# A PEER trunk layer on one core: the residual stage folded into the last expert group, four rows per group re-timed, and the gate-table stores issued by ScalarE

## The chip, the cores and the metric

One Trainium2 chip, one of its cores. The metric is device time in microseconds of one execution of the whole layer. TensorE (PE), VectorE (DVE), ScalarE (ACT), GpSimd (POOL) and SyncE (SP) run their own instruction streams and meet at semaphores; the 16 DMA engines move data between SBUF and DRAM.

## The reference, cut to what matters

The layer has two sub-layers. The first (two token mixers, merge, output projection) gives `x1`. The second is a PEER retrieval layer, and it is the one that the change touches:

```
h2   = rms_norm(x1) * (1 + scale2) + shift2
s    = (h2 @ w_query) . sub_keys           # 8 heads, 2 halves, 128 keys each
16 best of 16 x 16 sums per head -> experts, gate = softmax
act  = gelu(h2 . expert_u[experts])
y    = sum over the 128 chosen experts of gate * act * expert_v[expert]
out  = x1 + gate2 * y
```

There are 1024 tokens, D = 1024, and 16384 experts (128 x 128). `x1`, `out` and both expert tables are float32.

## The kernel before, in words

The 1024 tokens are 8 tiles of 128. Six of them (`DT` = 6, 768 tokens) are computed **densely**: for all 16384 experts, with a gate matrix that is zero where an expert was not chosen. The last two tiles (`FEW` = 2) are computed **sparsely**: each chosen expert's row is fetched by an indirect DMA (a gather of one 1024-wide row per token, 512 KB), in a ring of four buffers (`RING` = 4), 256 gathers of expert_u rows and 256 of expert_v rows.

**rows_phase (U part).** For each of 128 expert rows, PE multiplies the row's 128 experts with the 768 tokens (two halves, L534 to L536), ACT applies Gelu (L1623) into one buffer per half, and SP stores each half into the table `ahead` in DRAM (`Ahead.store`, L1590 to L1594). ACT may write a half's buffer again only when its store has landed (`ge_out`, L1620). Cutting of float32 operands into a high and a low part is done by ACT (`cut_high`, L1613) and DVE (`cut_low`, L1617); the row's expert_u is loaded by POOL (L1588), and POOL also issues the sparse gathers (L1539), whose dot products DVE takes (`dot_row`, L1556). DVE runs its steps in the order in which they are written: the low cut of the next row, then the dot products.

The phase has three stages, each with two rows or so per step: `tiles` (48 rows, routing beside them), `blocks` (24 rows in 12 blocks of 64 tokens) and `rest` (56 rows; the first 23 turns of two rows bring one batch of four gathers per row). In `blocks` the gate matrix is built: per group of four tokens DVE (L1913, L1917) and ACT (`last_row`, L1780, L1782) write one-hot rows, PE multiplies them (L1985), ACT copies the result to `stage` (L1805). After 16 groups the block's 4 MB, 16384 runs of 256 bytes, go to the DRAM table `gates` in one DMA (L1764). SP issues it, after the block's last two stores of `ahead`:

```
for j in range(ROWS_BLOCK):
    A.store(sp, ...)
sp.wait_ge(g_cp.sem, g_cp.done(b * NG + (NG - 1)))
sp.dma_start(gv[...], stage[...]).then_inc(st_out[half].sem, 16)
```

**expert_phase (V part).** 32 groups of four expert rows. Per group PE runs 12 units (6 token tiles x 2 halves of D), 12 matmuls each (L2147 to L2149). The even units add up in six held PSUM banks over all groups; the odd units go through two moving banks that DVE adds to `acc` (L2119). DVE also multiplies the next group's two tables (`gate`, L2097), cuts (`cut_v` L2101, `cut_H` L2105) and adds eight gathered rows per group (`add_row`, L1565) at the units of `ROW_AT`, every unit but 2, 5, 8 and 11. POOL gathers the rows. SP loads `expert_v`, `ahead` and `gates` (L2056, L2058, L2060). After the last group ACT copies the six held banks to `acc` (L2089).

**finish_phase.** A phase of its own: SP loads gate2 (broadcast, 512 KB) and the 8 tiles of x1, DVE multiplies and adds tile by tile (L2184, L2186; `Chain` makes each wait for the one before), SP stores each tile (L2176). Phases are separated by a barrier of all engines and the clearing of semaphores.

## Time and profile before

| what | us |
|---|---|
| median of 3 runs | 3766.74 |
| lowest and highest run | 3756.76, 3779.36 |
| the profiled execution, its own time | 3757.52 |
| its span, first to last instruction | 3755.6 |

Mean granted TensorE clock of the profiled execution: 0.953 of full speed. Busy shares of the span: PE 90%, DVE 69%, ACT 31%, POOL 23%.

How to read it: a row of the timeline is start, duration, engine, line of the kernel, operation, output <- inputs, count and, in brackets, the idle time before it and what ended it. "SPq" and "POOLq" rows are the issuing of DMAs, not the transfer. A table by stage gives, for each stretch, each engine's busy time, the granted clock, the DMA engines' mean share and GB/s.

### The profile page before, as it was taken

The page shows a single profiled execution, that of the slowest core. Times are in us where ns is not written, and L with a number is a line of the kernel's source. Part 1 is how long each engine was busy: PE and PEld are TensorE (multiplying, and loading weights), DVE is VectorE, ACT ScalarE, POOL GpSimd, SP SyncE. Part 2 cuts the span into 40 slices and gives each one's busy share as a digit, 9 for nine tenths or more (in the row PEclk, how much of TensorE's full clock was granted, in tenths as well). Part 3 has the DMA queues.
Part 4 walks back from the last instruction along what each step waited for, and adds up shares of the span by engine and source line. Part 5 has one row for each costly group of instructions (what it writes and reads, how often), then busy time and mean ns, then how long its engine had stood idle before and what let it go on. Part 6 is the DMA issues. An engine that isn't in the chain of part 4 may idle for free. (4 is left out here: it accounts for less than half of the span.)

```text
span 3755.6 us, 58665 instructions
## 1 busy us (share of the span) xinstructions
PE 3374.4 (90%) x18867; PEld 3068.5 (82%) x18867; DVE 2585.7 (69%) x4897; ACT 1174.2 (31%) x1966; POOL 873.0 (23%) x900
## 2 busy tenths in 40 slices
PE   5997999786579699999999899999699999999996
PEld 4997999774468599999899899999588888888885
DVE  6435777444358788888888756663577777777775
ACT  3004555321222223226777522222222222222220
POOL 1001111110000001112222257662233333333331
PEclk8998999897789899999999999999899999999998
DMA  6622222242211134445888999994687778778775
GB/s 248 218 88 93 88 88 73 93 125 88 84 54 44 37 123 142 151 155 160 236 235 238 262 308 342 337 332 175 243 296 288 284 287 295 283 283 294 289 284 196
DMA packets 436327, 745.41 MB, mean 198 GB/s; under 512 B 224304, under 2 KB 275680, under 8 KB 433120
## 3 DMA queue, kind: packets, MB, share of 16 engines
q1 hardware_dynamic: 337312, 375.61, 30.1%
q0 software_dynamic: 98304, 368.10, 28.3%
q8 instruction: 68, 1.11, 0.1%
q14 instruction: 67, 0.55, 0.0%
q10 hardware_dynamic: 576, 0.04, 0.0%
HBM read 610.44 MB, written 133.19 MB: 198 GB/s over the span
## 5 line engine op out<-in xcount | busy, mean ns | idle before, releaser
L534 PE MATMUL apab<-h2hi,auhib 128*128 128x384 f32 x2048 | 707.1, 345 | 65.5 <-DVEq L60 47.1
L536 PE MATMUL apab<-h2hi,aulob 128*128 128x384 f32 x2048 | 687.3, 336 | 0.0
L535 PE MATMUL apab<-h2lo,auhib 128*128 128x384 f32 x2048 | 687.3, 336 | 0.0
L1539 POOL DMA_INDIRECT vrow<-in_expert_v,fw_now x256 | 318.1, 1242 | 723.8 <-DVE acc L1565 710.7
L534 PEld LDWEIGHTS apab<-h2hi,auhib 128*128 128x128 f32 x2048 | 387.3, 189 | 75.4 <-ACT ageb L1623 36.6
L535 PEld LDWEIGHTS apab<-h2lo,auhib 128*128 128x128 f32 x2048 | 387.3, 189 | 0.0
L536 PEld LDWEIGHTS apab<-h2hi,aulob 128*128 128x128 f32 x2048 | 386.2, 189 | 0.0
L1623 ACT ACTIVATE ageb<-apab 128x384 f32<-128x384 f32 x256 | 125.7, 491 | 686.9 <-PE apab L536 663.5
L2147 PE MATMUL eheld<-vhi,Hhi 128*128 128x512 f32 x768 | 303.0, 395 | 32.4 <-DVE Hlo L2105 32.4
L1565 DVE SCALAR_TENSOR_TENSOR acc<-vrow,fw_share,acc 128x1024 f32<-128x1024 f32 x256 | 327.2, 1279 | 0.0
L1588 POOL DMA_DIRECT2D aurb<-in_expert_u x128 | 71.6, 560 | 1033.6 <-DVEq L60 709.6
L2119 DVE TENSOR_TENSOR acc<-acc,evo 128x512 f32<-128x512 f32 x192 | 132.1, 688 | 255.8 <-PE evo L2149 255.8
L2148 PE MATMUL eheld<-vlo,Hhi 128*128 128x512 f32 x768 | 300.1, 391 | 0.0
L2149 PE MATMUL eheld<-vhi,Hlo 128*128 128x512 f32 x768 | 299.4, 390 | 0.0
L2147 PE MATMUL evo<-vhi,Hhi 128*128 128x512 f32 x768 | 298.8, 389 | 0.0
L2148 PE MATMUL evo<-vlo,Hhi 128*128 128x512 f32 x768 | 298.8, 389 | 0.0
L2149 PE MATMUL evo<-vhi,Hlo 128*128 128x512 f32 x768 | 298.7, 389 | 0.0
L2081 ACT ACTIVATE Hhi<-gr 128x768 fp32r<-128x768 f32 x128 | 108.5, 848 | 604.6 <-DVE gr L2097 604.6
L1985 PE MATMUL gp<-grow,gcol 128*128 128x128 f32 x1536 | 208.6, 279 | 31.5 <-ACT grow L1782 16.4
L1985 PEld LDWEIGHTS gp<-grow,gcol 128*128 128x128 f32 x1536 | 198.3, 193 | 42.9 <-issue 28.8
L1617 DVE TENSOR_TENSOR aulob<-aurb,auhib 128x1024 fp32r<-128x1024 f32 x128 | 156.5, 1223 | 110.5 <-ACT auhib L1613 107.1
L1556 DVE SCALAR_TENSOR_TENSOR urow<-urow,nx 128x1024 f32<-128x1024 f32 x128 | 156.6, 1225 | 72.5 <-DMA urow<-in_expert_u_rows,fw_now 68.0
(295 smaller groups left out, 7419.1 us busy)
## 6 DMA issues: line engine op xcount, KB each, us to landing
aurb<-in_expert_u POOLq DMA_DIRECT2D x128, 512.0 KB, 4.3
vraw<-in_expert_v SPq DMA_DIRECT2D x128, 512.0 KB, 3.3
ahead_dram<-ageb SPq DMA_DIRECT2D x256, 192.0 KB, 3.6
gates_dram<-arena SPq DMA_DIRECT2D x12, 4096.0 KB, 24.0
ga<-ahead_dram SPq DMA_DIRECT2D x128, 384.0 KB, 5.3
gr<-gates_dram SPq DMA_DIRECT2D x128, 384.0 KB, 5.9
late<-in_w_ada SPq DMA_DIRECT2D x48, 512.0 KB, 6.3
gw<-in_w_in POOLq DMA_DIRECT2D x8, 1408.0 KB, 8.7
```

The source lines that it names most:

```text
L534: pe.matmul(out, lhi, rhi, start=(k == 0), stop=False)
L535: pe.matmul(out, lhi, rlo, start=False, stop=False)
L536: return pe.matmul(out, llo, rhi, start=False, stop=(k == n - 1))
L1539: pool.indirect_dma_start(self.ring[i], None, table, bass.IndirectOffsetOnAxis(ap=self.now[:, h, i:i + 1], axis=0)).then_inc(self.row_in[i ...
L1556: dve.scalar_tensor_tensor(self.ring[i], self.ring[i], 1.0, self.h2[:, i % FEW], ALU.mult, ALU.mult, accum_out=flat[:, bass.ds(n, 1)]).the ...
L1565: dve.scalar_tensor_tensor(at, self.ring[i], flat[:, bass.ds(n - ITEMS, 1)], at, ALU.mult, ALU.add).then_inc(self.row_used.sem, 1)
L1617: link(link.eng.tensor_tensor(self.ulo[:, p], self.ur[:, p], self.uhi[:, p].bitcast(F32), ALU.subtract), self.ulo_done.sem)
L1985: step = pe.matmul(pg[u][:, q], col[:, u * G + q], row[:, u * G + q], start=True, stop=True)
L2119: dve.tensor_tensor(place_of(u), place_of(u), vo[u // 2 % BANKS][:, :], ALU.add).then_inc(vo_add.sem, 1)
L2147: pe.matmul(bank[:, :], hi, vhi[:, m, ds], start=fresh, stop=False)
L2148: pe.matmul(bank[:, :], hi, vlo[:, m, ds], start=False, stop=False)
L2149: step = pe.matmul(bank[:, :], lo, vhi[:, m, ds], start=False, stop=(q == Q - 1 and (dh == 1 or final)))
```

## The change

Three edits. (1) `finish_phase` is gone. SP loads gate2 at the start of `expert_phase`, and x1 into buffers of tables that are free once the last group is cut (`x1_place`). In the last group DVE does, per half tile, the multiplication by gate2 (reading the held PSUM bank itself on even units) and the addition to x1 (`finish`), and the two sparse tiles after unit 5; SP stores each tile as it is done. ACT's six copies of held banks are gone. (2) The last 16 gathered rows: twelve are added in the last group but one (one at each unit), four in the last group (units 0 to 3), where it was eight and eight. (3) The 4 MB store of a block of `gates` moves from SP to ACT, between ACT's last copy to `stage` and its last Gelu of the block.

```diff
@@ rows_phase, sync
                             A.store(sp, b * 2 + (ROW_GATE + j), b * 2 + (ROW_GATE + j))
-                        sp.wait_ge(g_cp.sem, g_cp.done(b * NG + (NG - 1)))
-                        sp.dma_start(gv[:, :, bass.ds(b * BT, BT)],
-                                     stage[:, :, half * BT:(half + 1) * BT]).then_inc(st_out[half].sem, 16)
@@ rows_phase, scalar, block_rows
                                 A.gelu(act, r, 0)
+                        act.wait_ge(g_cp.sem, g_cp.done(b * NG + (NG - 1)))
+                        act.dma_start(gv[:, :, bass.ds(b * BT, BT)],
+                                      stage[:, :, half * BT:(half + 1) * BT]).then_inc(st_out[half].sem, 16)
                         A.gelu(act, b * 2 + (ROW_GATE + ROWS_BLOCK - 1), 1)
@@ expert_phase
+        gate2 = sb("gate2", [P, D])
+        FEW_AT = 5
+        LAST = [0, 1, 2, *range(DT, TT), *range(3, DT)]
-                    body(turn, p, False)
-            body(GROUPS // 2 - 1, 0, False)
-            body(GROUPS // 2 - 1, 1, True)
+                    body(turn, p, 0)
+            body(GROUPS // 2 - 1, 0, 1)
+            body(GROUPS // 2 - 1, 1, 2)
+        def x1_place(t):
+            held_by = (ga, gr, vr)[t // 3]
+            flat = held_by[:, :, :].rearrange("p s t -> p (s t)")
+            return flat[:, t % 3 * D:(t % 3 + 1) * D]
@@ sync
+                sp.dma_start(gate2[:, :], gate2_dram.to_broadcast([P, D])).then_inc(gate2_in, 16)
...
+                sp.wait_ge(vlo_done.sem, vlo_done.done(NKEYS - 1))
+                sp.wait_ge(Hlo_done.sem, Hlo_done.done(NKEYS - 1))
+                for t in (0, 1, *range(DT, TT), *range(2, DT)):
+                    sp.dma_start(x1_place(t), x1[t * P:(t + 1) * P, :]).then_inc(x1_in[t], 16)
+                for n, t in enumerate(LAST):
+                    sp.wait_ge(out_done, n + 1)
+                    sp.dma_start(out[t * P:(t + 1) * P, :], x1_place(t)).then_inc(out_sent, 16)
+                sp.wait_ge(out_sent, 16 * TT)
@@ scalar
-                act.wait_ge(acc_clear, 1)
-                for i in range(HELD):
-                    act.wait_ge(held_mm, (GROUPS - 1) * HELD + i + 1)
-                    act.activation(place_of(2 * i), held[i][:, :], ACT.Copy)
@@ vector
+                def finish(t, h, src):
+                    cols = slice(h * HALF, (h + 1) * HALF)
+                    link(dve.tensor_tensor(acc[:, t, cols], src, gate2[:, cols], ALU.mult))
+                    link(dve.tensor_tensor(x1_place(t)[:, cols], x1_place(t)[:, cols], acc[:, t, cols], ALU.add),
+                         *[out_done] * (h == 1))
+                    rows, first_row = (ROW_AT, p * EACH) if not near else (range(UNITS), 0) if near == 1 else (range(2 * EACH - UNITS), UNITS)
+                    last = near == 2
...
-                            dve.tensor_tensor(place_of(u), place_of(u), vo[u // 2 % BANKS][:, :], ALU.add).then_inc(vo_add.sem, 1)
-                        if u in ROW_AT:
-                            j = ROW_AT.index(u)
-                            few.add_row(dve, turn * (2 * EACH) + (ITEMS + p * EACH + j), j % RING, acc)
+                            add = dve.tensor_tensor(place_of(u), place_of(u), vo[u // 2 % BANKS][:, :], ALU.add)
+                            if last:
+                                link(add, vo_add.sem)
+                                finish(u // 2, 1, place_of(u))
+                            else:
+                                add.then_inc(vo_add.sem, 1)
+                        elif last:
+                            dve.wait_ge(held_mm, (GROUPS - 1) * HELD + u // 2 + 1)
+                            dve.wait_ge(x1_in[u // 2], 16)
+                            finish(u // 2, 0, held[u // 2][:, :])
+                        if u in rows:
+                            j = rows.index(u)
+                            few.add_row(dve, turn * (2 * EACH) + (ITEMS + first_row + j), j % RING, acc)
+                        if last and u == FEW_AT:
+                            dve.wait_ge(few.row_used.sem, few.row_used.done(2 * ITEMS - 1))
+                            for t in range(DT, TT):
+                                dve.wait_ge(x1_in[t], 16)
+                                for h in range(2):
+                                    finish(t, h, acc[:, t, h * HALF:(h + 1) * HALF])
+                dve.wait_ge(gate2_in, 16)
-def finish_phase(nc, acc, x1, gate2_dram, out, keep):
...
```

## Rows read from the trace of the kernel before

**Rows 1.** Timeline of VectorE from the last expert unit to the end.

```profile
3723.37 0.69 DVE L2119 TENSOR_TENSOR acc<-acc,evo 128x512 f32<-128x512 f32 x1 [2.36 <-PE evo L2149]
3730.42 1.23 DVE L2184 TENSOR_TENSOR acc<-acc,gate 128x1024 f32<-128x1024 f32 x1 [6.36 <-DMA gate<-mod_dram]
3731.87 1.23 DVE L2186 TENSOR_TENSOR fx<-fx,acc 128x1024 f32<-128x1024 f32 x1 [0.23 <-DMA fx<-x_dram]
3733.24 1.23 DVE L2184 TENSOR_TENSOR acc<-acc,gate 128x1024 f32<-128x1024 f32 x1
...
3750.31 1.23 DVE L2186 TENSOR_TENSOR fx<-fx,acc 128x1024 f32<-128x1024 f32 x1
```

**Rows 2.** Timeline of SyncE, same stretch: the eight issues of the output in one row.

```profile
3733.18 18.77 SPq L2176 DMA_DIRECT2D out<-fx  x8
```

**Rows 3.** Timelines of SyncE, ScalarE and TensorE after the last block of the gate table.

```profile
2135.84 0.38 SPq L1764 DMA_DIRECT2D gates_dram<-arena  x1
2139.38 25.75 SPq L1593 DMA_DIRECT2D ahead_dram<-ageb  x1
...
2167.55 0.98 ACT L1623 ACTIVATE ageb<-apab 128x384 f32<-128x384 f32 x2 [23.21 <-DMA ahead_dram<-ageb]
...
2168.09 0.69 PE L534 MATMUL apab<-h2hi,auhib 128*128 128x384 f32 x1 [16.91 <-ACT ageb L1623]
```

**Rows 4.** Stages table: busy us (instructions) of PE, PEld, DVE, ACT, POOL; PEclk, DMA share, GB/s.

```profile
2156.00:2168.00 12.00, 0.00 (x0) 0.00 (x0) 0.00 (x0) 0.46 (x1) 0.00 (x0) 0.52 1.09 319
2168.00:2176.00 8.00, 7.91 (x31) 7.92 (x32) 5.90 (x9) 2.02 (x4) 3.31 (x4) 0.65 0.45 132
2176.00:2196.00 20.00, 20.00 (x117) 20.00 (x116) 10.81 (x16) 4.06 (x7) 11.43 (x13) 1.00 0.88 289
2476.00:2496.00 20.00, 17.94 (x101) 17.13 (x100) 13.66 (x22) 4.78 (x8) 15.03 (x14) 1.00 0.96 336
```

**Rows 5.** GpSimd's index copy, one per batch: timeline (one row), source view 2171 to 2556 us.

```profile
2146.96 0.23 POOL L1532 COPY fw_now<-fw_index 128x4 uint32 x1
...
L1532 POOL COPY fw_now<-fw_index x43: 208/345/1012, 2172.1 to 2549.0; 128x4 uint32 x43
```

**Rows 6.** Waits in 2176 to 2556 us: who waited for whom, us in total, times, longest.

```profile
DVE urow L1556 <- DMA urow<-in_expert_u_rows,fw_now: 65.9, 60, 2.7
DVE nx L1556 <- DMA nx<-in_expert_u_rows,fw_now: 49.1, 79, 2.4
```

**Rows 7.** Timelines of VectorE around the start of the last expert group.

```profile
3679.76 0.69 DVE L2119 TENSOR_TENSOR acc<-acc,evo 128x512 f32<-128x512 f32 x1 [1.55 <-PE evo L2149]
...
3689.33 0.95 DVE L2105 TENSOR_TENSOR Hlo<-gr,Hhi 128x768 fp32r<-128x768 f32 x1
3690.64 0.69 DVE L2119 TENSOR_TENSOR acc<-acc,evo 128x512 f32<-128x512 f32 x1 [0.35 <-PE evo L2149]
3691.24 1.28 DVE L1565 SCALAR_TENSOR_TENSOR acc<-vrow,fw_share,acc 128x1024 f32<-128x1024 f32 x1
```

**Rows 8.** DMA issues: count, KB each, median us from issue to landing.

```profile
vraw<-in_expert_v SPq DMA_DIRECT2D x128, 512.0 KB, 3.3
gates_dram<-arena SPq DMA_DIRECT2D x12, 4096.0 KB, 24.0
vrow<-in_expert_v,fw_now POOLq DMA_INDIRECT x256, 5.6
```

**Rows 9.** Timelines of ScalarE and TensorE at the end of one block.

```profile
1822.92 0.60 ACT L1805 ACTIVATE arena<-gp 128x512 f32<-128x512 f32 x1 [1.33 <-PE gp L1985]
1823.96 0.49 ACT L1623 ACTIVATE ageb<-apab 128x384 f32<-128x384 f32 x1 [0.45 <-PE apab L536]
1825.70 1.15 PE L1985 MATMUL gp<-grow,gcol 128*128 128x128 f32 x8 [1.77 <-ACT grow L1782]
```

**Rows 10.** Timeline of SyncE after the first block's store.

```profile
1767.40 12.72 SPq L1593 DMA_DIRECT2D ahead_dram<-ageb  x1
```

**Rows 11.** Timeline of TensorE at the start of the V part.

```profile
2672.50 0.77 PE L2147 MATMUL eheld<-vhi,Hhi 128*128 128x512 f32 x1 [32.44 <-DVE Hlo L2105]
```

More of the change, by code:

```diff
@@ L1999, in _, with expert_phase @@
                 rest(pe, rest_rows)
-def expert_phase(nc, expert_v, gates, ahead, acc, few, keep):
+def expert_phase(nc, expert_v, gates, ahead, acc, few, x1, gate2_dram, out, keep):
     K = keep
@@ L2029, in expert_phase @@
         acc_clear = sem("acc_clear")
+        gate2 = sb("gate2", [P, D])
+        gate2_in, out_done, out_sent = sem("gate2_in"), sem("out_done"), sem("out_sent")
+        x1_in = [sem(f"x1_in{t}") for t in range(TT)]
+        FEW_AT = 5
+        LAST = [0, 1, 2, *range(DT, TT), *range(3, DT)]
         ROW_AT = [u for u in range(UNITS) if u % 3 != 2]
@@ L2105, in cut_H, with group @@
                     dve.tensor_tensor(Hlo[:, m], gr[:, m % GS], Hhi[:, m].bitcast(F32), ALU.subtract).then_inc(Hlo_done.sem, 1)
-                def group(turn, p, last):
+                def finish(t, h, src):
[3 more added lines that the diff above has]
+                         *[out_done] * (h == 1))
+                def group(turn, p, near):
                     g = turn * 2 + p
                     ahead_turn, ahead_p = (turn, 1) if p == 0 else (turn + 1, 0)
+                    rows, first_row = (ROW_AT, p * EACH) if not near else (range(UNITS), 0) if near == 1 else (range(2 * EACH - UNITS), UNITS)
+                    last = near == 2
                     for u in range(UNITS):
@@ L2118, in group @@
                             dve.wait_ge(vo_add.sem, vo_add.free(n))
-                            dve.tensor_tensor(place_of(u), place_of(u), vo[u // 2 % BANKS][:, :], ALU.add).then_inc(vo_add.sem, 1)
-                        if u in ROW_AT:
-                            j = ROW_AT.index(u)
-                            few.add_row(dve, turn * (2 * EACH) + (ITEMS + p * EACH + j), j % RING, acc)
+                            add = dve.tensor_tensor(place_of(u), place_of(u), vo[u // 2 % BANKS][:, :], ALU.add)
[17 more added lines that the diff above has]
+                                    finish(t, h, acc[:, t, h * HALF:(h + 1) * HALF])
+                link = Chain(dve, sem("dve_out"))
                 for q in range(Q):
@@ L2158, in _ @@
                 group(GROUPS // 2 - 1, 1, False, True)
-def finish_phase(nc, acc, x1, gate2_dram, out, keep):
-    with ExitStack() as ctx:
-        sem = ctx.enter_context(phase_semaphores(nc))
-        sb = lambda n, s, d=F32: ctx.enter_context(nc.sbuf_tensor(n, s, d))
-        gate = sb("gate2", [P, D])
-        xt = sb("fx", [P, TT, D])
-        gate_in, f_in, f_done, f_out = sem("gate_in"), [sem(f"f_in{t}") for t in range(TT)], sem("f_done"), sem("f_out")
-        with nc.Block() as block:
-            @block.sync
-            def _(sp):
-                sp.dma_start(gate[:, :], gate2_dram.to_broadcast([P, D])).then_inc(gate_in, 16)
-                for t in range(TT):
-                    sp.dma_start(xt[:, t], x1[t * P:(t + 1) * P, :]).then_inc(f_in[t], 16)
-                for t in range(TT):
-                    sp.wait_ge(f_done, t + 1)
-                    sp.dma_start(out[t * P:(t + 1) * P, :], xt[:, t]).then_inc(f_out, 16)
-                sp.wait_ge(f_out, 16 * TT)
-            @block.vector
-            def _(dve):
-                link = Chain(dve, sem("dve_finish"))
-                dve.wait_ge(gate_in, 16)
-                for t in range(TT):
-                    link(dve.tensor_tensor(acc[:, t], acc[:, t], gate[:, :], ALU.mult))
-                    dve.wait_ge(f_in[t], 16)
-                    link(dve.tensor_tensor(xt[:, t], xt[:, t], acc[:, t], ALU.add), f_done)
 class Keep:
@@ L2240, in program @@
         acc = sb("acc", [P, TT, D])
-        expert_phase(nc, io["expert_v"][0], gates, ahead, acc, few, K)
-        finish_phase(nc, acc, x1, io["mod_dram"][None, 5 * D:6 * D], out[0], K)
+        expert_phase(nc, io["expert_v"][0], gates, ahead, acc, few, x1, io["mod_dram"][None, 5 * D:6 * D], out[0], K)
 _INS = ["x", "c", "w_ada", "b_ada", "norm_mix_w", "w_in", "hg_lb_raw", "hg_norm_w", "q_norm_w", "k_norm_w", "sinks",
```

## The prediction, made before the changed kernel ran

> **What bounds the kernel now.** I read the end of the timeline first, because edit 1 works there. The last PE result reaches DVE at 3723.37, and the add ends at 3724.06. After that PE has no work: DVE waits 6.36 us for gate2, and then works through 16 chained operations of 1.23 us, to 3751.54 [rows 1]. SP issues the eight stores of the output from 3733.18 to 3751.95 [rows 2]; the span ends at 3755.6, so 4.1 us lie between DVE's last operation and the end. The tail after the matmuls is thus about 31.5 us, with DVE in most of it.
>
> Then I looked for what edit 3 touches, the 4 MB stores of the gate table. The last of them is issued by SP at 2135.84. SP's next DMA, the store of a Gelu result, begins its issue at 2139.38 and needs 25.75 us for it, where the issue of the 4 MB itself took 0.38. ACT then waits 23.21 us for the landing of that store, and PE 16.91 us for ACT [rows 3]. The granted clock falls in this wait from full speed (2.4 GHz) to 0.52 on average from 2156 on, in effect the 1.2 GHz level [rows 4], and PE's first matmul afterwards takes 0.69 us [rows 3]; over the next 8 us the clock is 0.65 on average, which costs PE 8 x (1 - 0.65), about 2.8 us more. So nearly 20 us of PE time hang on this one place. The same block of SP's queue follows each store (12.72 us after the first [rows 10]), but ACT shows no wait for it in the blocks, where a half's buffer is wanted again some 16 us later.
>
> Third, the stretch after it (2176 to 2556): DMA share 0.88 to 0.96 and 289 to 336 GB/s, PE busy 20 of 20 us at first and 17.94 of 20 later [rows 4]. Here the gathers set the pace, not PE: 43 batches start between 2172.1 and 2549.0, so 376.9 / 42 = 8.97 us a row [rows 5], and DVE waits 65.9 + 49.1 = 115 us in it for gathered rows [rows 6].
>
> **The change part by part.**
>
> *Removal of the finish phase.* The new last group is worked out on the old clock of the trace. Operations of 512 columns take 0.69 us [rows 7], a chained one starts 0.03 after the one before, or 0.13 where it also signals [rows 1] (3733.24 is 0.14 after the end before it). So an even unit costs 0.69 + 0.03 + 0.69 + 0.03 = 1.44, an odd one 0.82 for the add and 1.54 for the pair, 2.36. A gathered row costs 1.19 when the next operation follows at once. DVE's work: 6 x 1.44 + 6 x 2.36 = 22.8; four rows 4.8; the two sparse tiles 2 x 1.44 + 2 x 1.54 = 6.0. Sum 33.6 us, against 32.6 us that PE needs for the group (12 units of 2.72, from 3690.64 to 3723.37 in [rows 1, 7]). DVE becomes the bound of this group. It can start when the first held bank is complete (about 3693.5) and x1's first tile is in. SP waits for the last low cut, which ends at 3690.28 [rows 7], then issues; 512 KB by SP land in 3.3 us in this stage, two gathers beside it take 5.6 [rows 8], so x1 is in at 3694 to 3696; I take 3695. Then DVE ends at 3695 + 33.6 = 3728.6. I followed the units one by one: after unit 0 no matmul is late, the sparse tiles hold DVE to about 3717, and unit 7's add ends at 3719.3, before PE wants that bank for unit 11 at 3720.4, so PE is not held. Six stores go out before the end, and the last one needs its 4.1 us as now: 3732.7. Gain 3755.6 - 3732.7 = **22.9 us** (bounds 21 and 24.5, by x1's landing). ACT's six copies were never on the path.
>
> *gate2's load ahead of the first tables.* One more issue and 512 KB in front of loads for which ACT and DVE wait; PE's start at 2672.50 hangs on them [rows 11]. At 512 KB per 1.5 us (about 340 GB/s, [rows 4]) **1.5 us lost** (0 to 2).
>
> *Twelve rows in the last group but one.* The four more stand at units 2, 5, 8, 11. Before the add of units 3, 7 and 9 DVE idles 1.5 to 1.8 us (1.55 in [rows 7]), so 1.19 goes in; unit 5's row comes after an add and is made up by unit 7; unit 11's follows the last low cut (as the row at 3691.24 does now [rows 7]) and leaves DVE free at 3692.4, before the first held bank is complete. Their gathers land in 5.6 us [rows 8], and four slots are 10.9 us apart at one row per 2.72 us. POOL's queue holds nothing else. **0**, cover gone at most 1.2.
>
> *ACT issues the table store.* In a block's end ACT idles 0.45 between its last copy (to 1823.52) and the last Gelu at 1823.96; then come the one-hot rows for which PE waits 1.77 us [rows 9]. The issue needs the wait for its own copy, address arithmetic and 0.38 us, in all 0.6 to 0.75, so the Gelu and everything behind it slip by 0.15 to 0.45 us, 12 times: I take 0.3 each, **3.6 us lost** (1 to 6). The store itself starts 1.7 us sooner, which nothing waits for.
>
> *The stall after the last block.* If SP's store is no longer behind the 4 MB, ACT's wait goes. PE gets nearly 20 us back at most, but gathers are late next: the batch before this one began at 2146.96, so the next would start at 2146.96 + 8.97 = 2155.9 and not at 2172.1 [rows 5], so the paced stretch moves forward by 16.1 us and not more. And the 4 MB must still be moved: from 2156 to 2168 the DMA engines carried 12 us x 319 GB/s = 3.8 MB [rows 4], with POOL and DVE idle. That now lies beside gathers at a DMA share of 0.95; if all of it had to be paid again at 340 GB/s it would cost 11.3 us and leave 5. Between 5 and 16 I take **11 us gained**: a share over 1 in the first of [rows 4] says that the two kinds of traffic overlap in part.
>
> Sum: 22.9 - 1.5 - 0 - 3.6 + 11 = 28.8, call it 29. From the profiled execution's 3757.5 this gives 3728.5. That execution lies 9.2 us under the median 3766.7 of the three runs, so on the median's scale it is 3737.7. I forecast 3737.
>
> **A rule that speaks against edit 3.** What the trace shows is that an SP issue is held after an SP store of 4 MB [rows 3, 10]; it has no case of an SP issue behind a large store of ACT. The Trainium skill, page "DMA: Bandwidth & Descriptors", in "Queues, rings and completion order", says that SP and ACT each own one row of rings on the same 16 engines, but not a descriptor generator of their own; in "Issuing engines are not separate DMA queues" it adds that issuing from several engines saves only the sequencer's time. By that rule the sum would lack the 11 us but for the 1.7 of the earlier start. No row here shows whether it holds.
>
> **The rivals.**
>
> A. *SP stays held.* What blocks the issue is common to both queues. For it: the engines were full (share 1.09 in the first of [rows 4]). Against it: POOL's gathers were issued and landed during the block. Gain 22.9 - 1.5 - 3.6 + 1.7 = 19.5: 3747. Chance 0.28.
>
> B. *The whole stall comes back.* The table's 256-byte traffic slips into gaps, and the gathers do not feel it: 16 instead of 11 and an issue on ACT that hides (1 instead of 3.6): gain 22.9 - 1.5 - 1 + 16 = 36.4, 3730. Chance 0.12.
>
> C. *The last group runs late.* x1 lands after 3698, or chained operations on PSUM cost over 0.8: 24 x 0.15 = 3.6 us more and a PE held at unit 11, with SP held too: gain 12 to 15, 3753. Chance 0.05.
>
> D. *Slower: ACT is held as SP is now.* If ACT's issue itself waits for room, 11 to 12.7 us as in [rows 10], the one-hot rows of the next block stand behind it and PE with them: 12 x 11 = 132 us lost, about 3870. It decides from 2.5 us per block on, where 12 x 2.5 eats the 29. Against it: SP's own issue of the 4 MB took 0.38, and ACT's queue is empty each time, since a store lands in 24.0 [rows 8] and blocks are 34 us apart. Chance 0.04.
>
> **How the numbers follow.** The forecast's own case has chance 0.51; its range is 3757.5 - 36 to 3766.7 - 22, 3721 to 3745. B reaches down to 3757.5 - 40 = 3717, A up to 3766.7 - 15 = 3752. I give 3716 to 3756: A, B and most of C are in it, D is out. Less than 0.5% (19 us) can't be told from no change here. Faster by more: 0.51 + 0.12 + half of A, less a little for the spread of runs, 0.75; same 0.20 (half of A, C); slower 0.05.
>
> **What would show it.** In the profile after: no DVE operation of 1024 columns after the last matmul; end within 10 us of it; 24 plus 8 operations of 512 columns at 0.69; the first of them at 3695 on the old clock. ACT's Gelu at a block's end 0.15 to 0.45 later, PE's wait there 1.9 to 2.2. SP's first issue after the last table store under 1 us: then A is wrong. Copies of the batch index still 9 us apart: then gathers set the pace; at 8.3 the gain is 16 and not 11. An SP issue of 20 us or more right there makes my forecast wrong.

## The result, and the profile after

| | before | after |
|---|---|---|
| median | 3764.01 us (7 runs, 3756.76 to 3779.36) | 3738.62 us (7 runs, 3730.37 to 3746.28) |
| ratio to before | | 0.9928, 95% interval 0.9907 to 0.9948 |
| profiled execution | 3757.52, span 3755.6 | 3743.68, span 3741.6 |
| mean granted clock | 0.953 | 0.952 |

The change makes the layer 25.4 us faster by the medians. 3737 was forecast, with 3716 to 3756 as the range.

To see where it comes from, cut both spans at the same three marks: ACT's Gelu at the end of the first block and of the last, and PE's first matmul of the V part.

| stretch | before, us | after, us | difference |
|---|---|---|---|
| start to the first block's last Gelu (unchanged code) | 1755.6 | 1767.4 | +11.9 |
| the other eleven blocks | 379.0 | 385.8 | +6.8 |
| last block's last Gelu to the V part | 537.9 | 523.8 | -14.1 |
| V part to the end | 1083.1 | 1064.6 | -18.5 |
| span | 3755.6 | 3741.6 | -14.0 |

The first row is no effect of the change. Over the thirteen profiles that share this code and this mark (before, after and all experiments but one) it lies anywhere from 1755.6 to 1770.6. Without it, the changed stretches give 25.8 us, close to the 25.4 of the medians. The following readings are therefore taken against the marks and not against the span. The other stretches vary too between kernels that share their code: by 5 us in the blocks, 9 behind the last block and 1.6 in the V part.

**The end.** Timelines of the kernel after: VectorE, one row of TensorE, SyncE.

```profile
3695.34 0.69 DVE L2143 TENSOR_TENSOR acc<-acc,evo 128x512 f32<-128x512 f32 x1 [0.36 <-PE evo L2190]
3695.94 1.28 DVE L1565 SCALAR_TENSOR_TENSOR acc<-vrow,fw_share,acc 128x1024 f32<-128x1024 f32 x1
3701.60 0.69 DVE L2125 TENSOR_TENSOR acc<-eheld,gate 128x512 f32<-128x512 f32 x1 [4.38 <-DMA ga<-x_dram]
3702.32 0.69 DVE L2126 TENSOR_TENSOR ga<-ga,acc 128x512 f32<-128x512 f32 x1
...
3732.58 0.69 DVE L2125 TENSOR_TENSOR acc<-eheld,gate 128x512 f32<-128x512 f32 x1 [0.60 <-DVE gr L2126]
...
3735.60 0.69 DVE L2126 TENSOR_TENSOR gr<-gr,acc 128x512 f32<-128x512 f32 x1
...
3726.57 0.50 PE L2188 MATMUL evo<-vhi,Hhi 128*128 128x512 f32 x1 [1.26 <-DVEq L60]
...
3695.06 0.81 SPq L2076 DMA_DIRECT2D ga<-x_dram  x2
...
3728.12 8.59 SPq L2079 DMA_DIRECT2D out<-gr  x3
```

These answer to [rows 1, 2]. DVE's 1024-column operations after the matmuls are gone, and every new 512-column operation takes 0.69 us. The work of the last group is DVE's, as forecast, and runs from 3701.60 to 3736.29. What was not forecast is the 4.38 us before it: SP issues x1 at 3695.06, at once after the last low cut, and the first tile is there only at 3701.6. The reason is in the DMA issues of the window 3690 to 3712 us (count, KB each, median us to landing):

```profile
ga<-x_dram SPq DMA_DIRECT2D x3, 512.0 KB, 7.3
```

These are x1's tiles 0 to 2. SP issues eight such loads in 4.3 us, and they share the 16 engines; a lone load of 512 KB by SP lands in 3.3 [rows 8]. None of the eight issues takes over 0.68 us, though 4 MB are under way, in pieces of 4096 bytes.

From DVE's last operation to the end it is 5.3 us, and it was 4.1. The difference lies behind the last landing, where GpSimd clears the semaphores of the phase (L131). There are 31 in the last phase now, and there were 12. Source views, after and then before (ns: least, median, most):

```profile
L131 POOLq EVENT_SEMAPHORE_RANGE_CLEAR  x31: 37/38/43, 3739.4 to 3741.3; - x31
L131 POOLq EVENT_SEMAPHORE_RANGE_CLEAR  x12: 38/38/38, 3754.6 to 3755.3; - x12
```

The clears start 0.065 us apart, so nineteen more take 1.2 us.

**After the last block.** Timelines of ScalarE and SyncE, then all of SyncE's issues of the Gelu results (ns: least, median, most).

```profile
2152.74 0.39 ACTq L1812 DMA_DIRECT2D gates_dram<-arena  x1
2153.26 0.49 ACT L1623 ACTIVATE ageb<-apab 128x384 f32<-128x384 f32 x1 [0.68 <-ACT arena L1802]
...
2153.91 45.01 SPq L1593 DMA_DIRECT2D ahead_dram<-ageb  x12
```

```profile
L1593 SPq DMA_DIRECT2D ahead_dram<-ageb x256: 332/332/370, 1327.7 to 2644.0; - x128
```

The issue of 25.75 us [rows 3] is gone; none of the 256 takes over 0.370. ACT and PE show no wait there. Stages table (columns as in [rows 4]):

```profile
2153.00:2165.00 12.00, 12.00 (x71) 12.00 (x70) 7.12 (x10) 3.91 (x6) 6.49 (x7) 1.00 1.05 279
2165.00:2173.00 8.00, 8.00 (x48) 8.00 (x47) 4.14 (x7) 2.05 (x3) 3.00 (x4) 1.00 1.06 399
2173.00:2193.00 20.00, 20.00 (x117) 19.84 (x115) 13.81 (x21) 3.98 (x6) 13.12 (x14) 1.00 1.09 391
2476.00:2496.00 20.00, 18.24 (x104) 17.61 (x103) 12.72 (x19) 3.98 (x6) 15.84 (x14) 1.00 0.96 353
```

PE stays busy at full clock, and the DMA engines carry up to 399 GB/s while the table store runs beside the gathers. The store itself becomes slow there. Queue q10 is ScalarE's, and all but 16 of its packets are the store's 16384 runs of 256 bytes (packets, MB, share of 16 engines, for 2152.7 to 2177.7 and 2177.7 to 2212 us):

```profile
q10 hardware_dynamic: 10108, 2.59, 46.7%
q10 hardware_dynamic: 6292, 1.61, 20.6%
```

Its last packet starts 59 us after the issue, where the stores in the blocks need 26. The trace of this kernel has no landing for it, but in four kernels with the same store (early_x1, few_on_pool, rows_8_8, further) it lands after 61 to 68 us. early_x1, the twelve stores (least, median, most):

```profile
DMA to landing us min/median/max: 24.0/25.8/67.6
```

Nothing waits for this store until the end of the phase. The gathers still set the pace afterwards. GpSimd's index copies, one per batch (timeline, then the source view from 2155 us on):

```profile
2157.27 0.34 POOL L1532 COPY fw_now<-fw_index 128x4 uint32 x1
2165.22 0.23 POOL L1532 COPY fw_now<-fw_index 128x4 uint32 x1
2176.40 0.91 POOL L1532 COPY fw_now<-fw_index 128x4 uint32 x1
...
L1532 POOL COPY fw_now<-fw_index x45: 233/313/1160, 2157.3 to 2552.0; 128x4 uint32 x45
```

394.7 / 44 = 8.97 us a row, the very pace of [rows 5]. The third batch starts 23.1 us after the block's last Gelu (2153.26). Before, that Gelu stands at 2134.57 and the third batch at 2172.06, 37.5 us later. That is a shift of 14.4 us. For the fourth batch it is 16.1, and for the last of the stretch 15.6; the stretch gained 14.1, or 15.5 if the longer wait at the start of the V part is left out.

**Block ends and the start of the V part.** Timelines of ScalarE and TensorE.

```profile
1837.23 0.39 ACTq L1812 DMA_DIRECT2D gates_dram<-arena  x1
1837.75 0.49 ACT L1623 ACTIVATE ageb<-apab 128x384 f32<-128x384 f32 x1 [0.68 <-PE apab L536]
...
1839.49 1.15 PE L1985 MATMUL gp<-grow,gcol 128*128 128x128 f32 x8 [2.01 <-ACT grow L1779]
...
2677.05 0.76 PE L2188 MATMUL eheld<-vhi,Hhi 128*128 128x512 f32 x1 [33.78 <-DVE Hlo L2120]
```

Against [rows 9, 11]: the Gelu's idle time grows from 0.45 to 0.68 (it is 0.44 or 0.45 at all twelve block ends before, 0.68 to 0.72 after), PE's from 1.77 to 2.01, and PE's wait at the V part from 32.44 to 33.78.

### The profile page after: what moved, and what is told of

Same layout as the page of the kernel before. It is cut to its first block and busy times, and to the rows that moved or that the text cites. A ratio compares the mean times of both kernels' runs of the same rounds, so it can differ in the third digit from the quotient of the medians.

```text
span 3741.6 us, 58649 instructions
## 1 busy us (share of the span) xinstructions
PE 3388.4 (91%) x18867; PEld 3079.4 (82%) x18867; DVE 2591.3 (69%) x4913; ACT 1171.8 (31%) x1960; POOL 863.5 (23%) x900
## 5 line engine op out<-in xcount | busy, mean ns | idle before, releaser
L1985 PE MATMUL gp<-grow,gcol 128*128 128x128 f32 x1536 | 210.4, 281 | 32.4 <-ACT grow L1779 22.9
## 6 DMA issues: line engine op xcount, KB each, us to landing
gates_dram<-arena ACTq DMA_DIRECT2D x12, 4096.0 KB, 25.7
```

The costliest lines, as they stand in the source:

```text
L1985: step = pe.matmul(pg[u][:, q], col[:, u * G + q], row[:, u * G + q], start=True, stop=True)
```

## The experiments

Each ratio is to the kernel before, timed in the same round. Its median was 3771.97 us beside sp_stores, only_act_stores, last_store_on_act and last_store_twice, 3759.48 beside two_issues, last_store_late, early_x1 and few_on_pool, and 3758.76 beside the other four. So times of different rounds are compared by their ratios.

**The parts apart: sp_stores, only_act_stores.** The first is the kernel after with the table stores back on SP; the second is the kernel before with only this edit.

```diff
# sp_stores, against after; only_act_stores is the reverse, against before
@@ sync
+                        sp.wait_ge(g_cp.sem, g_cp.done(b * NG + (NG - 1)))
+                        sp.dma_start(gv[...], stage[...]).then_inc(st_out[half].sem, 16)
@@ scalar
-                        act.wait_ge(g_cp.sem, g_cp.done(b * NG + (NG - 1)))
-                        act.dma_start(gv[...], stage[...]).then_inc(st_out[half].sem, 16)
```

> The changed kernel with edit 3 undone (SP issues the table stores again). My account (the place after the last block is worth 15 us, the issue on ACT costs 3 to 7 in the blocks): 8 to 12 us slower than the changed kernel, so about 3748, ratio to the kernel before 0.9952; SP issue of some 25 us after the last table store, ACT wait of some 23 us, PE wait at a block's end back at 1.77 us. Rival (all of the gain is the finish phase, edit 3 gives and takes the same): no difference from the changed kernel, ratio 0.993.

> The kernel before with edit 3 alone. My account: 8 to 12 us faster than before, ratio 0.997 to 0.9975, tail after the last matmul unchanged at 31 us, no SP issue over 1 us after the last table store, rest stretch (end of the last block to PE's start of the V part) shorter by 15 us. Rival (nothing gained by the move): ratio 1.000.

| kernel | median (runs) | ratio to before, interval | blocks | last Gelu to V | V to end |
|---|---|---|---|---|---|
| before | | | 379.0 | 537.9 | 1083.1 |
| sp_stores | 3753.04 (12) | 0.9954, 0.9929 to 0.9979 | 379.7 | 533.7 | 1065.2 |
| only_act_stores | 3756.21 (12) | 0.9957, 0.9929 to 0.9985 | 385.2 | 523.2 | 1083.9 |
| after | 3738.62 (7) | 0.9928, 0.9907 to 0.9948 | 385.8 | 523.8 | 1064.6 |

Each part changes its own stretches and leaves the others alone. By the medians each is worth some 16 or 17 us (0.46% and 0.43%), with about 10 us to either side; together that is 0.89% against 0.72% for the whole, no contradiction within these intervals, and the marks are the finer measure. By them the store's move is worth less than its stall: it shortens the last stretch and lengthens the blocks, 8.5 us net between before and only_act_stores and 3.8 between sp_stores and after, and some 10 by the means of all kernels (below). sp_stores has the stall back (timelines of ScalarE and TensorE; SyncE's issues):

```profile
2176.86 0.97 ACT L1623 ACTIVATE ageb<-apab 128x384 f32<-128x384 f32 x2 [24.37 <-DMA ahead_dram<-ageb]
...
2177.40 0.69 PE L534 MATMUL apab<-h2hi,auhib 128*128 128x384 f32 x1 [18.07 <-ACT ageb L1623]
```

```profile
L1593 SPq DMA_DIRECT2D ahead_dram<-ageb x256: 332/332/26829, 1324.3 to 2646.5; - x128
```

**Only the last store matters: last_store_on_act.** ACT issues the last block's store alone, and SP the other eleven.

```diff
@@ sync: the last turn is written out, its last block without the store
@@ scalar
+                        if final and half == 1:
                             act.wait_ge(...)
                             act.dma_start(gv[...], stage[...])
```

> The changed kernel, but only the last block's store is issued by ACT, the eleven others by SP. If what the move costs in the blocks is the issue in front of ACT's last Gelu: PE's wait at a block's end 1.77 instead of 2.01 us, blocks shorter by 3 us, and the gain after the last block kept: 3 us faster than the changed kernel. If the longer intervals between blocks (35.6 to 36.1 us, five of eleven against two before) also come from the move: 7 us faster. If the last block's stall needs all stores off SP: 15 us slower.

3741.93 us (6 runs), ratio 0.9915 (0.9883 to 0.9947). The stretch behind the last block is 520.5 us, as short as with all twelve on ACT: the gain of edit 3 hangs on one store. SP's issues after the other eleven take up to 12.739 us again, and nothing waits for them. The blocks' stretch is no shorter (385.4 against 385.8), so this saves nothing that can be shown: PE's wait at every second block end is back at 1.77, and most intervals are the shorter ones, but one at the place where the last turn was written out is 37.7 us.

**What holds the issue: last_store_twice, two_issues.** The first adds, behind the last block's store, a second one of the same 4 MB to a spare table, also by ACT. It was meant to price the 4 MB beside the gathers. The second adds one DMA of 64 KB by ACT behind each table store.

```diff
# last_store_twice, after the last block's store
+                            act.dma_start(gv2[...], stage[...]).then_inc(twice, 16)
# two_issues, after every store
+                        act.dma_start(spare[...], K.ident[:, :]).then_inc(twice, 16)
```

> The changed kernel with the last block's 4 MB stored a second time, to a spare table. If bytes beside the gathers are paid in full (DMA share at its limit): the stretch from the last block to the V part grows by about 11 us. If the 256-byte traffic slips into gaps: by 0 to 3 us. Gathers' pace near 9 us a batch either way at the end of the stretch.

> The changed kernel with one more, small DMA (64 KB to a spare table) issued by ACT behind each table store. If the issue itself stands in the path of a block's end: PE's wait there grows from 2.0 to about 2.5 us, the blocks by 12 x 0.45 = 5 to 6 us. If the issue is hidden and what made the blocks longer is the table's traffic: no change of PE's wait at a block's end. The two 4 MB stores' landing (25.7 us) stays in both cases.

last_store_twice: 3757.25 us (10 runs), ratio 0.9973 (0.9948 to 0.9999). The stretch is 539.3 us, counted from where the Gelu would have stood without the second issue (from the Gelu itself it is 520.3). But the trace says that it did not measure bytes (timelines of ScalarE and TensorE):

```profile
2149.39 0.39 ACTq L1815 DMA_DIRECT2D gates_dram<-arena  x1
2149.81 18.99 ACTq L1818 DMA_DIRECT2D spare_dram<-arena  x1
2168.90 0.49 ACT L1623 ACTIVATE ageb<-apab 128x384 f32<-128x384 f32 x1 [19.54 <-issue]
...
2169.44 0.69 PE L534 MATMUL apab<-h2hi,auhib 128*128 128x384 f32 x1 [16.88 <-ACT ageb L1623]
```

ACT's own next issue was held for 18.99 us, and the Gelu behind it, and PE: the stall of before, on the other engine. It costs 15.5 us against the kernel after. As a price of 4 MB the run is void. two_issues shows that the size of the second DMA does not matter: 3973.86 us (4 runs), ratio 1.0570 (1.0549 to 1.0591). Tile view of the small DMA (ns: least, median, most), and PE's waits in the blocks (who waited for whom, us in total, times, longest):

```profile
L1817 ACTq DMA_DIRECT2D spare_dram<-ident x12: 18416/18622/19971, 1755.6 to 2360.4; - x12
```

```profile
PE gp L1989 <- ACT grow L1782: 229.8, 11, 21.6
PE apab L534 <- ACT ageb L1623: 16.8, 1, 16.8
```

Neither of the two cases expected came out. Twelve holds of 18.6 us are 223 us, and the profiled span is 225.9 us longer than after's (3967.5 against 3741.6). So in this kernel: after a 4 MB store of 16384 runs the engine that issued it can't issue its next DMA until that store has nearly landed (20.8 us here), while the other engine's issues stay short (SP's longest in this run is 0.371 us). This is the prediction's rival D, mechanism and all. It stayed away because ACT issues no DMA in the blocks but these, 34 us apart, and none behind the last one. Whether the size of the store or its number of runs makes the hold, no run separates. The eight loads of x1, 4 MB in pieces of 4096 bytes, were not held, which points at the runs.

**Do the 4 MB cost anything beside the gathers: last_store_late.** ACT issues the last block's store only after the 23 turns with gathers, at 2541.06.

```diff
@@ scalar: the last block without its store, then
+                with act.Fori(0, WITH) as turn:
+                    rest_rows(turn, False, True)
+                act.wait_ge(g_cp.sem, g_cp.done(NB * NG - 1))
+                act.dma_start(gv[:, :, (NB - 1) * BT:NB * BT], stage[:, :, BT:2 * BT])
```

> The changed kernel with the last block's table store issued by ACT only after the 23 turns that bring gathered rows, where the DMA share is 0.3. If the 4 MB beside the gathers are paid in full (as the second store was, 15 us): the stretch from the last block to the V part 10 to 15 us shorter than the changed kernel's 523.8 us, and the time 10 to 15 us less, ratio 0.989. If the gathers' pace is set by something else (GpSimd, latency) and the last store costs nothing there: no difference from the changed kernel.

3734.05 us (6 runs), ratio 0.9931 (0.9916 to 0.9946); the stretch is 518.3 us. In the seven kernels with the store in its place it lies between 517.0 and 525.8 (mean 522.0), so at most some 4 us are the store's, and by the ratios nothing (0.9931 against 0.9928). The third batch starts 21.9 us after the Gelu and not 23.1 (mean of the seven); the next four batches start 1.5 to 2.3 us earlier than the mean of the seven. So some 2 us is what the rows show for the 4 MB beside the gathers. The price is small because the store is stretched over 59 us or more there; issued late, it lands in 29.6.

**Do the gathers set how much comes back: no_gathers_act, no_gathers_sp.** Both leave out the gathered expert_u rows behind the blocks, and so their part of the output.

```diff
@@ gpsimd, rest turns
-                            few.gather_all(pool, table, batch, p, batch * RING)
+                            few.gather_none(...)     # loads 16 columns into the same buffer
@@ vector
-                                few.dot_row(dve, ..., i)
+                                few.dot_row(dve, ..., i, 0.0)     # multiplies by 0
```

> Left out: the gathered rows of expert_u in the stage after the blocks. Each gather there becomes a load of 16 columns into the same buffer, and the dot product multiplies by 0, so the output lacks these rows; the instructions, their order and their waits are the same. ScalarE issues the table stores, as in the kernel after. The question is whether the gathers' pace set how much of the stall came back. My theory: without the gathers' 512 KB each PE sets the pace, the stretch from the last block's last Gelu to PE's first matmul of the V part falls from 523.8 to about 505 us, and against no_gathers_sp it is shorter by the whole PE stall, 19 to 20 us. Rival: the gathers have nothing to do with it; the difference to no_gathers_sp is again 14 us.

> Left out: the gathered rows of expert_u in the stage after the blocks, as in no_gathers_act, and SyncE issues the table stores, as in the kernel before. My theory: SP's issue behind the last store is still 25 us long, PE is idle 17 to 18 us behind it, and the stretch from the last block's last Gelu to PE's first matmul of the V part is 524 to 526 us, 19 to 20 more than in no_gathers_act. Rival: the issue is held for less time where no gathers are in the queues (under 15 us), which would say that gathers and not the store itself hold it; or the difference to no_gathers_act is again 14 us.

3706.04 us (4 runs) and 3720.09 us (4 runs); ratios 0.9851 (0.9826 to 0.9877) and 0.9886 (0.9859 to 0.9913). The stretch is 498.7 us with ACT's stores and 509.7 with SP's. Expected were about 505 and 524 to 526. My number for the difference, 19 to 20 us, was wrong, because the stall itself shrank; the hold is neither the 25 us of my theory nor under the 15 of the rival. no_gathers_sp, timelines of ScalarE and TensorE, and SyncE's issues:

```profile
2173.30 1.02 ACT L1631 ACTIVATE ageb<-apab 128x384 f32<-128x384 f32 x2 [14.60 <-DMA ahead_dram<-ageb]
...
2173.85 0.69 PE L534 MATMUL apab<-h2hi,auhib 128*128 128x384 f32 x1 [8.30 <-ACT ageb L1631]
```

```profile
L1601 SPq DMA_DIRECT2D ahead_dram<-ageb x256: 332/332/17769, 1331.1 to 2625.5; - x128
```

Two things follow. The hold is 17.8 us and not 26.8 when the gathers are out: it lasts about as long as the store takes to drain, and that depends on the traffic beside it (this store lands 22.5 us after its issue and the hold ends after 21.3; in sp_stores 31.4 and 29.5). And against a PE stall of 8.3 us plus about 1.5 for the lower clock behind it (0.82 over 8.1 us), the whole of it comes back: 11.0 us, of which 0.8 stands in PE's wait at the V part. With the gathers in, about 20 us of stall give 14, or 15 without the wait at the V part. The third batch moves forward by 14.4 us with gathers (37.5 to 23.1 us after the Gelu) and by 8.4 without (28.9 to 20.5). So without gathers nothing is missing from what PE lost. With them some 5 us are, and what comes back is as much as the batches moved. One pair without gathers, and stretches that vary by up to 9 us with them: this fits the account that the gathers' pace limits what comes back, but the 5 us are rough and don't show it by themselves. A load of 16 columns in place of a gather also takes another path of issue, so the pair changes more than bytes.

**The late x1: early_x1.** x1's tiles 0 to 2 are issued once DVE has multiplied the last two tables (L2112); their buffer (`ga`) is free from then on, two steps before the last low cut. The two sparse tiles are issued one wait earlier as well, before that for the last low cut of the table.

```diff
@@ expert_phase, sync
+                sp.wait_ge(H_done.sem, H_done.done(NKEYS - 1))
+                for t in range(3):
+                    sp.dma_start(x1_place(t), x1[t * P:(t + 1) * P, :]).then_inc(x1_in[t], 16)
                 sp.wait_ge(vlo_done.sem, vlo_done.done(NKEYS - 1))
```

> The changed kernel, with x1's tiles 0 to 2 loaded as soon as the table that holds their place has been multiplied (H), not after the last low cuts. If VectorE bounds the last group and its start waits for x1: first operation on a held bank about 3 us after the last add of the group before (now 6.26), the 1.26 us that PE waits for a moving bank gone, end 3 to 4 us earlier. Rival (the end is set by PE and the last store): the same end, the gap only moves.

3725.91 us (5 runs), ratio 0.9906 (0.9889 to 0.9924). Timelines of SyncE and VectorE:

```profile
3670.53 1.31 SPq L2075 DMA_DIRECT2D ga<-x_dram  x3
...
3676.57 0.69 DVE L2148 TENSOR_TENSOR acc<-acc,evo 128x512 f32<-128x512 f32 x1 [0.35 <-PE evo L2195]
...
3679.40 0.69 DVE L2130 TENSOR_TENSOR acc<-eheld,gate 128x512 f32<-128x512 f32 x1 [0.94 <-PE eheld L2195]
```

The first finishing operation starts 2.83 us after the start of the last add and not 6.26, and waits for PE's held bank, no longer for a DMA. PE is no longer held at unit 11. The V part is 1062.3 us, 2.3 shorter: most of the 3.4 arrives at the end. The other 1.1 is lost before the last group, where that add stands 1019.4 us after PE's first matmul and not 1018.3; why, no run tells. That the median lies 13 us under the kernel after's can't be put down to this edit: the marks give it 2.3 us, the two were not timed side by side, and the intervals of their ratios overlap.

**The sparse tiles on GpSimd: few_on_pool.** GpSimd does the last multiplication and addition of the two sparse tiles, as operations of 1024 columns, and DVE none of them.

```diff
+                    plink(pool.tensor_tensor(acc[:, t], acc[:, t], gate2[:, :], ALU.mult))
+                    plink(pool.tensor_tensor(x1_place(t), x1_place(t), acc[:, t], ALU.add), few_out)
@@ vector
-                        if last and u == FEW_AT:
-                            ...
```

> The changed kernel with the two sparse tiles' four multiplications and additions (1024 columns each) on GpSimd in the last group. If VectorE's own work is the bound there (34.7 us of chained operations): 6 us less on it, then PE's last unit sets the end, 4 to 6 us earlier. Rival (GpSimd and VectorE take each other's time on SBUF): VectorE's 512-column operations take over 1 us while GpSimd works, and the end comes no earlier or later than in the changed kernel.

3727.06 us (4 runs), ratio 0.9916 (0.9891 to 0.9941), but the V part is 1065.0 us against 1064.6: six microseconds of DVE work are gone and nothing is gained. Timelines of VectorE and GpSimd:

```profile
3699.97 0.68 DVE L2135 TENSOR_TENSOR acc<-eheld,gate 128x512 f32<-128x512 f32 x1
3700.20 2.38 POOL L2097 TENSOR_TENSOR acc<-acc,gate 128x1024 f32<-128x1024 f32 x1 [15.64 <-DVE acc L1565]
3700.69 2.45 DVE L2136 TENSOR_TENSOR ga<-ga,acc 128x512 f32<-128x512 f32 x1
3702.66 2.73 POOL L2098 TENSOR_TENSOR vraw<-vraw,acc 128x1024 f32<-128x1024 f32 x1
3703.17 0.69 DVE L2153 TENSOR_TENSOR acc<-acc,evo 128x512 f32<-128x512 f32 x1
3704.01 1.93 DVE L2135 TENSOR_TENSOR acc<-acc,gate 128x512 f32<-128x512 f32 x1 [0.16 <-DVE acc L2153]
3705.98 2.77 DVE L2136 TENSOR_TENSOR ga<-ga,acc 128x512 f32<-128x512 f32 x1
```

While GpSimd works, DVE's four operations of 512 columns with both inputs in SBUF take 1.86 to 2.77 us and not 0.69; those with one input in PSUM (`eheld`, `evo`) stay at 0.69. The four lose 6.25 us together, just what was taken off DVE: from its first finishing operation to its last it takes 34.4 us, against 34.7 in the kernel after. The Trainium skill, page "GPSIMD Engine Reference", section "8. Key points", says that GpSimd shares its SBUF interfaces with VectorE and contends with instructions that have two SBUF inputs; the trace agrees, by the operand.

**Edit 2 alone: rows_8_8.**

```diff
-        FEW_AT = 5
+        FEW_AT = 7
...
-                    rows, first_row = (ROW_AT, p * EACH) if not near else (range(UNITS), 0) if near == 1 else (range(2 * EACH - UNITS), UNITS)
+                    rows, first_row = (ROW_AT, p * EACH) if near < 2 else (range(EACH), EACH)
```

> Edit 2 undone in the kernel after: the last 16 gathered rows stand eight and eight again, so the last group has four rows more (the sparse tiles follow after unit 7), and DVE bounds it. My theory: DVE's work in the last group is four rows of 1.19 us = 4.8 us more, 39.5 instead of 34.7 us from the first finishing operation to the last, and the stretch from PE's first matmul of the V part to the end is 1064.5 + 4.8 = 1069.3 us; PE is held in the last group, but nothing waits for that. The group before has idle time before its adds again (1.5 us and not 0.4). Rival: with more time between their gathers or with PE's pace as the cover the four rows are free, and the stretch is again 1064.5 us within 1; then edit 2 was needless.

3735.93 us (4 runs), ratio 0.9936 (0.9907 to 0.9966): the median can't show it. The marks do. From the first finishing operation to the last it takes 39.6 us (39.5 expected, 34.7 after), and the V part 1070.6 (1069.3 expected, 1064.6 after). Edit 2 is worth 5 to 6 us; the prediction had it inside the 22.9.

**Further than the change: further.** early_x1, with rows of twelve, twelve and none in the last three groups, the sparse tiles after unit 3, and gate2 loaded behind the first tables.

```diff
-        FEW_AT = 5
+        FEW_AT = 3
...
+                    rows, first_row = {0: (ROW_AT, p * EACH), 3: (range(UNITS), EACH), 1: (range(UNITS), 2 * EACH - UNITS), 2: ((), 0)}[near]
```

> A version meant to go further than the kernel after. x1's tiles 0 to 2 are loaded once, as soon as the last high part of H is read (as in early_x1); the rows of the last three groups are twelve, twelve and none; gate2 is loaded behind the first tables. My theory: DVE's work in the last group is 22.8 + 6.0 = 28.8 us, less than the 32.6 us that PE needs, so PE bounds the group and the end comes about 2.4 us earlier than in early_x1 against PE's first matmul of the V part: about 1060 us instead of 1062.3; and PE's idle time at the start of the V part is 32.4 instead of 33.8 us. In all 5 us less than the kernel after, of which the medians can show little: 3733 us. Rival: the twelve rows in two groups in a row run out of gathers (the ring has four buffers) and hold DVE's adds and PE by more than is gained, shown by DVE's waits on vrow before L1565.

3726.51 us (6 runs), ratio 0.9908 (0.9882 to 0.9935). The V part takes 1059.9 us (1060 expected), and PE's wait at its start is 32.45 again. DVE shows no wait for a gather in the two groups of twelve. Timeline of VectorE in the last group:

```profile
3689.86 0.69 DVE L2132 TENSOR_TENSOR acc<-eheld,gate 128x512 f32<-128x512 f32 x1 [0.99 <-issue]
...
3692.58 0.69 DVE L2152 TENSOR_TENSOR acc<-acc,evo 128x512 f32<-128x512 f32 x1 [1.30 <-PE evo L2198]
...
3698.02 0.69 DVE L2152 TENSOR_TENSOR acc<-acc,evo 128x512 f32<-128x512 f32 x1 [1.36 <-PE evo L2198]
...
3721.50 0.69 DVE L2133 TENSOR_TENSOR gr<-gr,acc 128x512 f32<-128x512 f32 x1
```

DVE waits for PE up to 3698; from then on, with the sparse tiles first, it is never idle for over 0.23 us. So the total came out as expected and its reason did not: DVE, not PE, still bounds the second half of the group. Moving the sparse tiles earlier is not the remedy; they would have to be spread over the units. That wasn't tried. This version has the shortest V part of all (4.7 us less than the kernel after), and is faster than the kernel before. That it beats the kernel after is not shown by the times: the intervals of the two ratios overlap.

## Why the prediction was right

The mechanism was the one forecast: DVE bounds the last group, and SP's issue is free once the table stores are ACT's. That the time was 1.6 us from the forecast is in part luck. The forecast took 29 to 30 us off 3766.7; measured are 25.4 off 3764.0. Two terms were off and partly cancel, and two small ones were close.

- **Removal of the finish phase, 22.9 forecast: 18.5 measured** (V part, 1083.1 to 1064.6), outside the bounds of 21 to 24.5. The step that failed is "512 KB by SP land in 3.3 us in this stage, two gathers beside it take 5.6": eight loads go out together, x1's tiles 0 to 2 land in 7.3, and DVE starts 6.3 us after the start of the last add where 4.4 was forecast: 1.9 us. DVE's chain took 34.7 and not 33.6: most links that also signal leave 0.15 to 0.23 us and not 0.13, and one leaves 0.60, which nothing explains: 1.1 us. From DVE's last operation to the end it is 5.3 us and not 4.1: 1.2 us. These are the nineteen more semaphores that the last phase clears. The forecast sign of an end within 10 us of the last matmul was missed: it is 12.0. "PE is not held" was wrong by 1.26 us at unit 11, exactly the bank named; nothing depended on it.
- **gate2's load, 1.5 forecast: 0.7 on average.** PE's wait at the V part is 32.42 to 32.45 where the load isn't ahead (before, only_act_stores, further), and with it anything from 31.5 (sp_stores) to 34.5 (two_issues), 33.1 in the mean of eleven kernels. The 1.3 of the profiled pair is one draw of these.
- **Twelve rows in the last group but one, 0 forecast: 0.** DVE still idles 0.36 us before the add at 3695.34, the tightest kind of place, and PE is not delayed.
- **ACT's issue, 3.6 forecast: 4.0.** Mean of the blocks' stretch over the seven kernels that have all twelve stores and nothing more on ACT (no_gathers_act is one), 383.0 us (380.5 to 385.8); over three with SP's, 379.0 (378.3 to 379.7). The mechanism forecast gives over half of it: 0.39 us of issue, the Gelu 0.23 later, PE's wait up by 0.24 [rows 9], over eleven intervals 2.6 us. The rest lies in how many intervals are 35 to 37 us long and not 34, for which no run gives the cause.
- **The stall after the last block, 11 forecast: 14.** Mean of the stretch over seven kernels 522.0 (after, only_act_stores, last_store_on_act, early_x1, few_on_pool, rows_8_8, further), over before and sp_stores 535.8; the pair of before and after alone gives 14.1. Without PE's wait at the V part the means differ by 15 us, and so do the places of the last batch. Right was the bound, 16.1 us by the place of the next batch, and that PE's 20 us are not the measure (the pair without gathers points the same way). The term that was mis-sized is "11.3 us if all of it had to be paid again": the 4 MB beside the gathers cost some 2 us by the batches (last_store_late). The store gave way instead, over 59 us, and the engines went from 336 to 391 and 399 GB/s with both kinds of traffic at once. The DMA share of 0.95 was no sign that they were full.

The rivals: A fell with SP's longest issue, 0.370 us. The Trainium skill, page "DMA: Bandwidth & Descriptors", section "Issuing engines are not separate DMA queues", says that issuing from several engines saves only the sequencer's time to initiate. Read literally it held, since the transfer itself is no faster (median 25.7 us to landing on ACT, 24.0 on SP); but this time is 25.75 us here and not 0.38, so the conclusion drawn from it, that the 11 us would not come back, was wrong. B was half right: the gathers hardly feel the store, but the bound of 16 isn't reached. C did not come true: the first tile of x1 is in at 3701.6, which is 3696.9 on the old clock (the add before it stands at 3695.34 and at 3690.64), later than the forecast's 3694 to 3696 but short of C's 3698, and no operation takes over 0.69. D is shown to be real by two_issues.

## What to carry to other kernels

A 4 MB store of 16384 small runs blocked the next DMA of the engine that issued it until it had nearly drained; size and number of runs were not separated. Put such a store on an engine that issues nothing else for that time, which beside other heavy traffic can be 60 us and not 25, and look for its victims not at its own issue (0.38 us) but at the one behind it in the queue. Where a stall is removed, ask what stream is late next (here the gathers, at 8.97 us a batch), and read the gain from how far that stream moves. Loads that are issued in one go must be priced together, not by a lone one's landing.

## What the runs showed that I had not expected

- The hold belongs to the issuing engine, is the same for a next DMA of 64 KB (18.6 us) or of 4 MB (19.0), and lengthens with the traffic beside the store: 17.8 us after the last block without gathers, 25.7 and 26.8 with them. In SP's other blocks it is 6.4 to 12.7 us. SP's next issue comes 2.7 to 14.2 us after the store and ACT's at once, so that all of these end 19 to 30 us after the store's own issue.
- The last store took 59 to 67 us to drain beside the gathers in all seven kernels with it on ACT and nothing behind it, and nobody felt it. In the kernel before, PE, DVE and GpSimd stood still for 12 us of that time, and it was through after 31. A second DMA by ACT within that time might be held as long; that wasn't tried.
- DVE's fp32 operations with two SBUF inputs slowed from 0.69 to as much as 2.77 us beside GpSimd's, so six microseconds handed to GpSimd gave nothing.
- The stretch before the first block varies by 15 us between kernels that share its code. One profile of each kernel can't show a change of 10 us in the span; marks around the changed stretch can.
